# Banded attention's projections and norms placed inside the stick-breaking stage, and latent attention's spreading products put in another order

## The reference, cut to what matters

```python
proj = h @ w_in[l]
c_q, c_kv, k_pe, q_s, k_s, v_s, qkv_sb = _split_cols(proj, IN_SIZES)
# latent attention, 6 heads of 64 + 32 features
qa = rms_norm_2((rms_norm_2(c_q, q_a_norm[l]) @ w_uq[l]).reshape(B, S, 6, 96), mla_q_norm[l])
ka = rms_norm_2(concat([k_nope, k_pe_h], axis=-1), mla_k_norm[l])
o_a = mla_attention(rope(qa), rope(ka), va)
# banded attention, 6 query heads, 2 key heads of 64
qb = rms_norm_2(q_s.reshape(B, S, 6, 64), swa_q_norm[l])
kb = rms_norm_2(k_s.reshape(B, S, 2, 64), swa_k_norm[l])
o_b = swa_attention(qb, kb, vb, positions, sinks[l], rel_bias)
# stick-breaking attention, 4 heads of 64
z = einsum('bqhd,bkhd->bhqk', qi, k) * scale
log_not = where(mask, log_sigmoid(-z), 0.0)
after = cumsum(log_not, axis=3, reverse=True) - log_not
a = where(mask, exp(log_sigmoid(z) + after), 0.0)
o_c = a @ v
```

## Time and profile before

| what | value |
|---|---|
| three runs | 4061.51, 4065.52, 4067.29; median 4065.52 |
| the profiled execution | 4065.02, its span 4063.2 |
| PE busy | 3838.8 (94%) |
| DVE busy | 1888.4 (46%) |
| ACT busy | 1479.9 (36%) |
| POOL busy | 1593.4 (39%) |
| mean granted clock of PE | 0.978 of full speed |

### The profile page before, as it was taken

How to read it: one execution, slowest core, us unless ns; L and a number is a source line. 1 busy time by engine, 2 the same in 40 slices (tenths; PEclk the granted TensorE clock), 3 DMA queues, 4 the chain that set the end, 5 groups by cost and what they waited for, 6 DMA issues and landing times.

```text
span 4063.2 us, 52410 instructions
## 1 busy us (share of the span) xinstructions
PE 3838.8 (94%) x19256; PEld 3034.3 (75%) x19256; DVE 1888.4 (46%) x3264; ACT 1479.9 (36%) x2293; POOL 1593.4 (39%) x786
## 2 busy tenths in 40 slices
PE   6987899999998899999999999999999999899999
PEld 5876688888775678887888753788878877547887
DVE  3775866543635566654554855222232232452222
ACT  3264532222335663334222554422232233533222
POOL 1320243444330036554554421455455553115554
PEclk9999999999999999999999998999999999989999
DMA  7610134442110026663665220233323332102332
GB/s 250 195 37 24 53 116 138 144 135 62 42 47 19 1 76 218 217 217 106 225 225 178 80 57 1 68 95 96 98 84 98 96 97 63 42 1 85 101 98 73
DMA packets 460501, 411.94 MB, mean 101 GB/s; under 512 B 28096, under 2 KB 405312, under 8 KB 460352
## 3 DMA queue, kind: packets, MB, share of 16 engines
q1 hardware_dynamic: 457903, 408.65, 32.5%
q10 hardware_dynamic: 2448, 1.32, 0.1%
HBM read 406.25 MB, written 7.60 MB: 102 GB/s over the span
## 4 chain that ended last, share of the span: by engine, by line
PE 56%; issue 17%; POOL 13%; DVE 8%; ACT 5%; DMA 1%; POOLq 0%; ACTq 0%; DVEq 0%; SPq 0%
PE psum L239 15%; PE psum L240 14%; PE psum L241 14%; POOL s_wlo L225 10%; PE psum L1645 2%; POOL s_alo L1365 2%; PE psum L1656 1%; ACT s_t L1693 1%; PE psum L1633 1%; PE psum L1624 1%; DVE s_stat L1760 1%; DVE s_t L1770 1%; POOL s_rstd L694 1%; DVE s_h L817 1%; PE psum L2553 1%
## 5 line engine op out<-in xcount | busy, mean ns | idle before, releaser
L225 POOL TENSOR_TENSOR s_wlo<-s_raw,s_whi 128x1024 fp32r<-128x1024 f32 x490 | 1180.8, 2418 | 1913.6 <-ACT s_whi L217 1912.1
L239 PE MATMUL psum<-s_xhi,s_whi 128*128 128x512 f32 x3264 | 1229.0, 377 | 22.6 <-POOL s_wlo L225 12.2
L240 PE MATMUL psum<-s_xlo,s_whi 128*128 128x512 f32 x3264 | 1221.8, 374 | 0.0
L241 PE MATMUL psum<-s_xhi,s_wlo 128*128 128x512 f32 x3264 | 1218.6, 373 | 0.0
L217 ACT ACTIVATE s_whi<-s_raw 128x1024 fp32r<-128x1024 f32 x490 | 510.3, 1056 | 1525.0 <-PE psum L241 1520.8
L239 PEld LDWEIGHTS psum<-s_xhi,s_whi 128*128 128x128 f32 x3264 | 616.9, 189 | 143.1 <-POOL s_wlo L225 14.8
L240 PEld LDWEIGHTS psum<-s_xlo,s_whi 128*128 128x128 f32 x3264 | 616.5, 189 | 111.5 <-issue 3.3
L241 PEld LDWEIGHTS psum<-s_xhi,s_wlo 128*128 128x128 f32 x3264 | 615.7, 189 | 112.3
L239 PE MATMUL psum<-s_ahi,s_whi 128*128 128x512 f32 x1232 | 469.1, 381 | 11.7 <-DVE s_y L1331 7.2
L241 PE MATMUL psum<-s_ahi,s_wlo 128*128 128x512 f32 x1232 | 465.4, 378 | 0.0
L240 PE MATMUL psum<-s_alo,s_whi 128*128 128x512 f32 x1232 | 462.6, 375 | 0.0
(11 more groups left out here) (311 smaller groups left out, 4245.0 us busy)
## 6 DMA issues: line engine op xcount, KB each, us to landing
s_ada_raw<-w_ada SPq DMA_DIRECT2D x224, 512.0 KB, 4.0
s_raw<-w_gu SPq DMA_DIRECT2D x176, 512.0 KB, 3.8
s_raw<-w_up SPq DMA_DIRECT2D x88, 512.0 KB, 4.7
s_raw<-w_dn SPq DMA_DIRECT2D x88, 512.0 KB, 3.5
s_raw<-w_down SPq DMA_DIRECT2D x44, 512.0 KB, 4.6
s_raw<-w_in SPq DMA_DIRECT2D x30, 512.0 KB, 3.9
s_raw<-w_in_ab SPq DMA_DIRECT2D x20, 512.0 KB, 6.4
s_area<-w_first SPq DMA_DIRECT2D x16, 512.0 KB, 11.8
```

The costliest lines, as they stand in the source:

```text
L225: pool.tensor_tensor(K.wlo[:, c % HL, 0:a * b], K.raw[:, c % RAW, 0:a * b], K.whi[:, c % HL, 0:a * b].bitcast(F32), ALU.subtract).then_inc ...
L239: pe.matmul(out, lh, rh, start=first, stop=False)
L240: pe.matmul(out, lh, rl, start=False, stop=False)
L241: return pe.matmul(out, ll, rh, start=False, stop=last)
```

## The change

- `HeadNorm` for banded attention goes away as a phase of its own. A new phase `WindowNorm`, listed behind `Stick`, has the same four tiles. Its parts are called from `Stick`'s queues: on PE tile 0 stands ahead of the first logits, tile 1 behind the second, tiles 2 and 3 behind the fourth, with the sums between them; ACT and DVE have the corresponding parts between `softplus` and `positive` of the first pair.
- Its tiles use PSUM banks 4 and 5, its sums banks 6 and 7. The root is made by Ln and Exp instead of Abs_reciprocal_sqrt, and the Newton steps work in PSUM.
- Both `hold` calls of `Stick` (24 and 18 products) are gone. The first `values` waits for the last window norm's reading.
- The SBUF places of `Stick`'s two pairs are exchanged.
- In `MlaNorm` the ten products of `spread` have another order, and the intermediate of the refinement is in PSUM instead of SBUF.

The hunk that only adds the semaphore names is left out.

```diff
--- before.py
+++ after.py
@@ -1813,7 +1813,7 @@
 
     def __init__(self, K, T, tiles, start=None, chunks=()):
         self.T, self.tiles, self.start = T, tiles, start
-        self.rq, self.rtmp, self.groups = K.rq, K.rtmp, None
+        self.rq, self.rtmp = K.rq, K.rtmp
         self.order = []
         for i in range(len(tiles) + 2):
             self.order += [(kind, j) for kind, j in (("tile", i), ("sum", i - 1), ("rot", i - 2))
@@ -1867,8 +1867,6 @@
                 e.wait_ge(self.sem["qn_ready"], self.at("qn_ready", j + 1))
                 ins = e.matmul(out[0:f, 0:TX], t["rope"][0], t["dst"][:, 0:TX], start=True, stop=True)
             ins.then_inc(self.sem["out_ready"], 1)
-            if self.groups and i == 0:
-                self.groups.sums(e)
 
     def first(self, e):
 
@@ -2189,7 +2187,7 @@
     PLACE = [0, 512, 896, 1152]
 
     def __init__(self, K, heads):
-        self.heads, self.pairs = heads, len(heads) // 2
+        self.heads, self.pairs, self.window = heads, len(heads) // 2, None
         super().__init__(K)
 
     def counts(self):
@@ -2220,9 +2218,8 @@
 
     def pe(self, e):
         K = self.K
-        e.wait_ge(self.sem["bias_ready"], self.at("bias_ready"))
-        e.wait_ge(self.sem["gn_ready"], self.at("gn_ready"))
-        self.hold(e, 24)
+        window = self.window
+        window.tile(e, 0)
         self.drained(e)
         e.wait_ge(self.sem["table_in"], self.at("table_in"))
 
@@ -2254,16 +2251,25 @@
             if kt == 3:
                 ins.then_inc(self.sem["so_ready"], 1)
 
-        for kt in range(4):
-            if kt == 2:
-                self.hold(e, 18)
-            logits(0, kt)
+        logits(0, 0)
+        logits(0, 1)
+        window.tile(e, 1)
+        window.sum(e, 0)
+        logits(0, 2)
+        logits(0, 3)
+        window.tile(e, 2)
+        window.sum(e, 1)
+        window.tile(e, 3)
+        window.sum(e, 2)
+        window.sum(e, 3)
         for p in range(self.pairs):
             for kt in range(4):
                 if p + 1 < self.pairs:
                     logits(p + 1, kt)
                 weights(p, kt)
                 if kt > 0:
+                    if p == 0 and kt == 1:
+                        e.wait_ge(self.sem["wn_read"], window.at("wn_read", 4))
                     values(p, kt - 1)
                 elif p > 0:
                     values(p - 1, 3)
@@ -2296,8 +2302,19 @@
             a = (6 + p % 2) * BANK
             e.activation(self.heads[2 * p][3], self.K.pf[:, a:a + BANK], ACT.Copy).then_inc(self.sem["st_done"], 1)
 
-        for kt in range(4):
-            softplus(0, kt)
+        window = self.window
+        window.keep(e, 0)
+        softplus(0, 0)
+        softplus(0, 1)
+        window.keep(e, 1)
+        window.guess(e, 0)
+        softplus(0, 2)
+        softplus(0, 3)
+        window.keep(e, 2)
+        window.guess(e, 1)
+        window.keep(e, 3)
+        window.guess(e, 2)
+        window.guess(e, 3)
         for p in range(self.pairs):
             for kt in range(4):
                 if p + 1 < self.pairs:
@@ -2329,13 +2346,113 @@
                 e.wait_ge(self.sem["a_ready"], self.at("a_ready", 8 * p + 2 * kt + j + 1))
                 e.tensor_tensor(d, d, K.before[:, :], ALU.add).then_inc(self.sem["lg_ready"], 1)
 
-        for kt in range(4):
-            positive(0, kt)
+        window = self.window
+        positive(0, 0)
+        positive(0, 1)
+        window.norm(e, 0)
+        positive(0, 2)
+        positive(0, 3)
+        for j in range(1, 4):
+            window.norm(e, j)
         for p in range(self.pairs):
             for kt in range(4):
                 if p + 1 < self.pairs:
                     positive(p + 1, kt)
                 masked(p, kt)
+
+
+class WindowNorm(Phase):
+    def __init__(self, K, tiles, chunks, groups):
+        self.tiles, self.groups, self.ring_T = tiles, groups, None
+        self.rq = K.rq
+        super().__init__(K)
+        self.c0 = len(K.chunks)
+        for j, (w, col, n) in enumerate(chunks):
+            up_chunk(K, w, col, self.at("out_ready", j + 1), n)
+        self.c_next = len(K.chunks)
+
+    def counts(self):
+        n = len(self.tiles)
+        return dict(out_ready=n, wn_kept=n, wn_sq=n, wn_sum=n, wn_ln=n, wn_r=n, wn_read=n, qn_ready=n)
+
+    def place(self, j):
+        return self.K.pf[:, (4 + j % 2) * BANK:(5 + j % 2) * BANK]
+
+    def total(self, j):
+        return self.K.pf[:, (6 + j % 2) * BANK:(7 + j % 2) * BANK]
+
+    def square(self, j):
+        return self.K.t1[:, :, :].rearrange("p a t -> p (a t)")[:, j % 2 * TX:j % 2 * TX + TX]
+
+    def sp(self, e):
+        for j in range(len(self.tiles)):
+            load_chunk(self.K, e, self.c0 + j)
+
+    def tile(self, e, j):
+
+        K = self.K
+        if j < 2:
+            e.wait_ge(self.sem[f"out_free{4 + j}"], self.at(f"out_free{4 + j}"))
+        else:
+            e.wait_ge(self.sem["wn_kept"], self.at("wn_kept", j - 1))
+        w = chunk_ops(K, e, self.c0 + j)
+        for k in range(8):
+            ins = three(e, self.place(j), [x[:, k, :] for x in w], (K.xhi[:, k, 0:TX], K.xlo[:, k, 0:TX]), k == 0, k == 7)
+        ins.then_inc(self.sem["out_ready"], 1)
+        if j == 0:
+            self.groups.sums(e)
+
+    def sum(self, e, j):
+
+        if j < 2:
+            e.wait_ge(self.sem["gn_ready"], self.at("gn_ready"))
+        else:
+            e.wait_ge(self.sem["wn_read"], self.at("wn_read", j - 1))
+        e.wait_ge(self.sem["wn_sq"], self.at("wn_sq", j + 1))
+        e.matmul(self.total(j), self.tiles[j]["sum"], self.square(j), start=True, stop=True).then_inc(self.sem["wn_sum"], 1)
+
+    def keep(self, e, j):
+
+        dst = self.tiles[j]["dst"]
+        split_hi(self.K, e, self.c0 + j + HL)
+        e.wait_ge(self.sem["out_ready"], self.at("out_ready", j + 1))
+        e.activation(dst, self.place(j), ACT.Copy).then_inc(self.sem["wn_kept"], 1)
+        e.wait_ge(self.sem["wn_kept"], self.at("wn_kept", j + 1))
+        if j >= 2:
+            e.wait_ge(self.sem["wn_sum"], self.at("wn_sum", j - 1))
+        e.activation(self.square(j), dst, ACT.Square).then_inc(self.sem["wn_sq"], 1)
+
+    def guess(self, e, j):
+
+        r = self.rq(j, TX)
+        e.wait_ge(self.sem["wn_sum"], self.at("wn_sum", j + 1))
+        if j >= 2:
+            e.wait_ge(self.sem["qn_ready"], self.at("qn_ready", j - 1))
+        e.activation(r, self.total(j), ACT.Ln, bias=self.K.eps[:, 0:1], scale=1.0 / self.tiles[j]["n"]).then_inc(self.sem["wn_ln"], 1)
+        e.wait_ge(self.sem["wn_ln"], self.at("wn_ln", j + 1))
+        e.activation(r, r, ACT.Exp, scale=-0.5).then_inc(self.sem["wn_r"], 1)
+
+    def norm(self, e, j):
+
+        K, t, x, r = self.K, self.tiles[j], self.total(j), self.rq(j, TX)
+        n = t["n"]
+        e.wait_ge(self.sem["wn_r"], self.at("wn_r", j + 1))
+        e.scalar_tensor_tensor(out=x, in0=x, scalar=n * EPS, in1=r, op0=ALU.add, op1=ALU.mult).then_inc(K.sem["dve_step"], 1)
+        e.wait_ge(K.sem["dve_step"], K.step())
+        e.scalar_tensor_tensor(out=x, in0=x, scalar=-0.5 / n, in1=r, op0=ALU.mult, op1=ALU.mult).then_inc(K.sem["dve_step"], 1)
+        e.wait_ge(K.sem["dve_step"], K.step())
+        e.scalar_tensor_tensor(out=r, in0=x, scalar=1.5, in1=r, op0=ALU.add, op1=ALU.mult).then_inc(self.sem["wn_read"], 1)
+        e.wait_ge(self.sem["wn_read"], self.at("wn_read", j + 1))
+        e.scalar_tensor_tensor(out=t["dst"], in0=t["dst"], scalar=t["gain"], in1=r, op0=ALU.mult,
+                               op1=ALU.mult).then_inc(self.sem["qn_ready"], 1)
+
+    def pool(self, e):
+        for j in range(len(self.tiles)):
+            split_lo(self.K, e, self.c0 + j + HL)
 
 
 class MixNorm(Phase):
@@ -2473,8 +2590,8 @@
         self.order = [("qp", 0), ("qp", 1), ("rot", 0), ("qn", 0), ("kn", 0), ("rot", 1), ("qn", 1), ("kn", 1),
                       ("rot", 2), ("qn", 2), ("kn", 2)]
         self.tiles = [x for x in self.order if x[0] != "rot"]
-        self.spread = [("qn", 0), ("kn", 0), ("qp", 0), ("kp", 0), ("qn", 1), ("kn", 1), ("qn", 2), ("kn", 2),
-                       ("qp", 1), ("kp", 1)]
+        self.spread = [("qn", 0), ("qn", 1), ("qn", 2), ("kn", 0), ("kn", 1), ("kn", 2), ("qp", 0), ("qp", 1),
+                       ("kp", 0), ("kp", 1)]
         super().__init__(K)
 
     def counts(self):
@@ -2599,7 +2716,7 @@
             if j in (3, 5):
                 self.mix.apply(e, j // 5)
         e.wait_ge(self.sem["r0_ready"], self.at("r0_ready", 1))
-        total, r, tmp = self.sums(), K.rstd[0:96, 0:TX], self.tmp
+        total, r, tmp = self.sums(), K.rstd[0:96, 0:TX], self.sums()
         e.scalar_tensor_tensor(out=tmp, in0=total, scalar=96 * EPS, in1=r, op0=ALU.add, op1=ALU.mult).then_inc(K.sem["dve_step"], 1)
         e.wait_ge(K.sem["dve_step"], K.step())
         e.scalar_tensor_tensor(out=tmp, in0=tmp, scalar=-0.5 / 96, in1=r, op0=ALU.mult, op1=ALU.mult).then_inc(K.sem["dve_step"], 1)
@@ -2925,8 +3042,8 @@
```

(15 more changed lines are left out.)

## The result

The changed kernel takes 4021.29 (median of four runs, 4018.27 to 4026.79), the kernel before 4064.12 (four runs, 4061.51 to 4067.29): ratio 0.9898, 95% interval 0.9884 to 0.9912, a gain of 42.8. The forecast was 4032, a gain of 32.8; the time lies in the range. The profiled execution was the longest of the four, 4026.79 with a span of 4024.5.

What follows compares the result with a forecast made beforehand. The kernel was taken as one serial chain of stages, 56% TensorE. Stick stage 11.0 plus spread 5.4 made 16.4 per layer, 32.8 for both layers; 4065.0 - 32.8 = 4032, range 4014 to 4048.

Steps and rivals of the forecast that it cites:

- The stick stage: First part, window tiles woven into stick-breaking: 12.1 gained, minus 0.4 and 0.7, so 11.0 per layer, bounds 6 and 13.
- A+11.1: Stick stage times count from A, the start of GroupNorm's three sums; logits (0,2) were forecast 11.5 after it.
- POOL's bias work: Stick stage: POOL forms the band's bias after the last norm, slowing masks in the loop; minus 0.4 per layer.
- the low stretch over tile 2: Stick stage: a low-clock stretch of 3.4 over tile 2 would cost 1.7, of which about 0.7 was taken.
- B: Rival, stick stage: ACT becomes the bound or the clock falls over both tiles; 6 instead of 11 per layer, 4042; 17%.
- D: Rival, stick stage: without fillers the clock stays low until Attn's fillers; 60 us low gives 12 more per layer, 4088; 4%.
- The spread: Second part, end of MlaNorm: earlier start and regrouped products at 1.2 GHz, Attn at 2496.7 against 2502.13; 5.4 per layer.
- six slots of 1.71: Spread: at 1.2 GHz the products take six slots of 1.71 plus some 0.6 for shape changes, from 2484.95 to 2495.8.
- case A: Rival, spread: clock stays at 2.4 GHz, Attn 9.0 earlier and some 3 gained inside it, 4019; 17%.
- The intermediate in PSUM: MlaNorm: Newton steps with PSUM operands aren't slowed beside POOL, so the spread starts 1.6 earlier.
- C: Rival, spread: the row groups don't overlap by threes, so the second part gives about nothing, 4043; 8%.
- Sixty-four rows beside 32: Spread: 64- and 32-row products taken one by one, four times 1.7; side by side the part would be 8.0 per layer.

Runs made afterwards that it cites:

- the repeat: The changed kernel run once more, unaltered, against the kernel before: 4024.68, ratio 0.9901.
- the weave alone: The changed kernel with MlaNorm's spread order and Newton intermediate as before, so only the window tiles inside the stick stage: 4043.58, ratio 0.9945.
- the order alone: The kernel before with only the new order of the ten spreading products: 4057.2, ratio 0.9979.
- the kernel with the tail filled: The changed kernel with 64-row spreading products next to each other and six filler products behind the last spreading product: 4026.03, ratio 0.9905.
- PSUM alone: The kernel before with only the intermediate of MlaNorm's Newton steps moved to PSUM: 4054.32, ratio 0.997.

## Why the prediction was right, and where it was short

**The stick stage: right, and step by step.** Logits (0,2) came at A+11.1 (forecast 11.5), (0,3) at 13.4 (13.8), behind holes of 0.32 and 1.55 (0.9 and 1.6). Keep 3 ended at 28.2 (28.4), the last norm at 35.3 (35.5), positive (1,0) at 36.9 (37.2), the second mask right behind. ACT's holes are the two named, one table load of 1.28 serves all, and POOL's bias work met the loop's masks (1.59 for a pair). The stage gained 12.2 and 9.9. Of the difference 1.6 is the low stretch over tile 2 in one layer (weights at 33.05 instead of 31.44), the size forecast for it; the rest lies behind the weights, where layers without a low stretch differ by as much (67.4 to 68.6 for the stage). Mean 11.05 against 11.0, and 10.55 in the repeat. That the hole of 1.55 causes that stretch is likely and not shown: with it the level fell over tile 2 in five of ten layers, one in each of five profiles (four times layer 1, in the weave alone layer 0), always 13.9 to 14.2 behind the first record of GroupNorm's sums; with the hole filled it fell in none of four. At one in two, four such layers in a row come by chance once in sixteen. B, a starved stage, did not come. What sets the two layers of one execution apart is not settled. D was wrong in its premise (the full tile that follows brought the level back, 1.00 again in 3425 to 3429) and in its price: where PE waits, a low level costs little (an eighth of a microsecond for each).

**The spread: the step that failed** is "So at 1.2 GHz: 2484.95, six slots of 1.71". The products ran at 2.4 GHz, case A with 17%, the premise right in the forecast's own words ("since PE's hole before it shrinks"). I had held against it that 32- and 64-row products did not lift a low level; but nothing had to be lifted. It had to be kept, and the two kernels with one edit each show by what: with the hole of 2.41 it fell, with 0.63 it held at the start. A's other reason, that three row groups work at once, did not keep it: the order alone has them and ran low. Spread and norm end gave 8.1 + 1.9 = 10.0 per layer instead of 5.4, twice 4.6 more. Case A's own sum was 9.0 plus 3 in `Attn`. The first term was a little small, since ten multiplies without a gap take 6.06 and not 6.9. The second failed: the level fell at `Attn`'s start, and latent attention took 0.6 to 2.0 longer than before, not 3 less: the mean granted clock over it was 0.90 in both layers before, 0.86 and 0.89 in the first profile, 0.86 in both layers of the repeat. Why the level falls just there is not settled. `Attn`'s own narrow products are not needed for it, since in layer 1 it fell before the first of them; fillers ahead of them moved the fall in one layer, and did not remove it.

So the time, 4021, lies outside my own forecast's spread of 4024 to 4038 and beside A's 4019, and that A's number is so near is in part luck: its sum had 1.0 per layer too little in the spread, nothing for banded attention, and 3 in latent attention that turned into a loss.

**Other terms.** The intermediate in PSUM was costed right: 0.69 a step, a hole of 0.63 (forecast 0.8), the spread 1.8 earlier (1.6). C did not come: three 32-row groups do overlap (six products in 1.92). Sixty-four rows beside 32 did not, as I had chosen: the slots are 1.05 instead of 0.86 at 2.4 GHz, 2.0 instead of 1.71 at 1.2. The Trainium skill (TensorEngine Tiling (Array Packing), key properties) says that a change of tiling mode drains the engine; the trace agrees, at about 0.2 (2.4 GHz) and 0.3 (1.2 GHz) per changed slot. By that rule the sorted order should gain, and its products did end sooner; what the rule can't tell is that DVE was the limit.

**The sum**, from the repeat's profile (span 4023.1, 40.1 under before's): per layer 10.55 in the stick stage (68.5 / 70.0), 10.05 in norm end and spread (36.9 and 7.4), 1.15 in banded attention (32.8 / 32.7), and 1.85 lost in latent attention (58.7 / 58.9): 19.9, twice 39.8. Against the forecast's 16.4 the spread gave 4.65 more, the stick stage 0.45 less, and the two attentions took 0.7 back. Banded attention takes what its clock allows: 33.9 at a mean granted clock of 0.90 before, 32.8 and 32.7 at 0.95 in the repeat, 36.6 at 0.81 and 34.0 at 0.90 in the first profile, and 32.2 at 1.00 in layer 1 of the kernel with the tail filled. Why its low stretch is now mostly the shorter one is not settled.

## What to carry to other kernels

Two chains that lie one behind the other and need different engines can be woven by hand, and a schedule worked out from single rows, instruction by instruction, held here within 0.5 us over 37. Here the hole ahead of a stage decided whether it began at the high level: before costing a stage at the level that the old trace shows, ask whether the change shortens that hole, since the same products then cost about half (1.05 against 2.0 for a slot of the spread). And before filling a hole to keep a level, see whether PE limits anything behind it: 14 to 17 us more at the low level cost 2 where PE waited.

## What was not expected of the hardware

- Moving one intermediate from SBUF to PSUM sped up both sides: DVE's step from 1.63 to 0.69, and POOL's five subtractions beside it from 7.10 to 6.27 (7.10 with the order alone, 6.24 with PSUM alone).
- A level that holds at a stage's start need not hold to its end: the PSUM edit alone gave spreads of 9.1 and 12.0 in the two layers of one execution, with the same hole of 0.63 ahead, and with both edits it fell inside the spread in one layer of fourteen (8.6 instead of 7.4).
- In the changed kernel the level falls within some two microseconds of `Attn`'s first product, in front of it or behind it, around a hole of 1.23. Six full products in that hole put the fall off to about 2495, thirteen microseconds on, and latent attention took 56.9 in that layer instead of 58.7 to 59.0. In the other layer of the same execution the level had fallen inside the spread, and the two stages took 2.2 more than in the repeat (8.6 and 60.0 against 7.4 and 58.9).
